# Gated linear attention by groups of tokens with projections as three rounded products, and low levels of a recurrence as 64-column tiles

## The reference

```
# HGRN2: per head, b = cumsum(log_f) in a chunk
scores[t, s] = sum_k q[t, k] * exp(b[t, k] - b[s, k]) * k[s, k]   for s <= t
o = scores @ v + (q * exp(b)) @ S
S = S * exp(b_last)[:, None] + (k * exp(b_last - b)).T @ v

# GLA, chunks of 64 tokens: u = h @ w_in
log_a = log_sigmoid(glr @ gate_up + bias) / 16        # glr: 16 columns of u
b = cumsum(log_a);  q_in = q * exp(b);  k_in = k * exp(-b);  k_st = k * exp(b_last - b)
scores = where(causal, q_in @ k_in.T, 0)
o = scores @ v + q_in @ S;   S = S * exp(b_last) + k_st.T @ v
out = o * rsqrt(mean(o * o) + eps) * norm_w * silu(g)
```

## Time and profile before

| | us |
|---|---|
| median of 3 runs | 4200.08 (4197.79 to 4201.01) |
| profiled execution | 4198.82, its span 4197.5 |
| PE busy | 3830.7 (91%) |
| DVE, ACT, POOL busy | 2019.6, 1521.5, 985.8 |
| mean granted clock of TensorE | 0.962 |

### The profile page before, as it was taken

One profiled execution on the slowest core, in us unless ns is written; L12 is line 12 of the kernel. 1 busy time (PEld: TensorE's weight loads), 2 busy tenths in 40 slices (PEclk: granted clock), 3 DMA queues, 4 the chain that ended last, 5 costly groups with the idle time before them and its releaser, 6 DMA issues.

```text
span 4197.5 us, 73047 instructions
## 1 busy us (share of the span) xinstructions
PE 3830.7 (91%) x30496; PEld 2853.2 (68%) x30496; DVE 2019.6 (48%) x4533; ACT 1521.5 (36%) x2905; POOL 985.8 (23%) x1018
## 2 busy tenths in 40 slices
PE   7999979896999998999997969999999979999989
PEld 4565558685877877878776857776777754655567
DVE  4665552354555555555553346666665651222222
ACT  3444441222444444444443334444444321122132
POOL 0000001232444443444432232322222200000032
PEclk9999989998999999999998989999999989999889
DMA  3000000222101101010103321111111120010032
GB/s 120 22 1 1 1 16 26 85 86 72 36 26 32 30 27 30 25 36 26 31 11 125 131 86 40 37 43 37 38 42 37 38 95 22 0 31 1 0 116 90
DMA packets 186549, 183.36 MB, mean 44 GB/s; under 512 B 6496, under 2 KB 158320, under 8 KB 186224
## 3 DMA queue, kind: packets, MB, share of 16 engines
q1 hardware_dynamic: 186224, 178.69, 13.4%
HBM read 145.12 MB, written 33.55 MB: 43 GB/s over the span
## 4 chain that ended last, share of the span: by engine, by line
PE 80%; DVE 9%; ACT 6%; issue 2%; DMA 2%; POOL 1%; SPq 0%; ACTq 0%; DVEq 0%; POOLq 0%
PE bank L193 15%; PE bank L195 14%; PE bank L194 14%; PE bank L1598 6%; PE bank L1169 4%; PE bank L447 4%; ACT arena L187 3%; PE bank L1655 3%; PE bank L2071 2%; DVE arena L685 1%; PE bank L2082 1%; ACT L277 1%; DVE arena L178 1%; PE bank L487 1%; PE bank L1698 1%
## 5 line engine op out<-in xcount | busy, mean ns | idle before, releaser
L194 PE MATMUL bank<-hT_cut,arena_cut 128*128 128x512 f32 x1824 | 725.3, 398 | 0.0
L187 ACT ACTIVATE arena<-bank 128x512 f32<-128x512 f32 (+1 forms) x584 | 313.0, 569 | 970.9 <-PE bank L195 450.8
L187 ACT ACTIVATE arena<-arena 128x512 f32<-128x512 f32 (+3 forms) x690 | 359.3, 549 | 283.8 <-POOL arena L1352 221.3
L193 PE MATMUL bank<-hT_cut,arena_cut 128*128 128x512 f32 x920 | 424.7, 462 | 8.9 <-DVE hT_cut L1409 8.9
L194 PEld LDWEIGHTS bank<-hT_cut,arena_cut 128*128 128x128 f32 x1824 | 351.2, 193 | 68.3 <-issue 15.2
L188 ACT ACTIVATE arena<-arena 128x256 f32<-128x256 f32 (+2 forms) x336 | 210.1, 626 | 511.6 <-DVE arena L177 276.6
L195 PE MATMUL bank<-hT_cut,arena_cut 128*128 128x512 f32 x920 | 366.5, 398 | 0.0
L193 PE MATMUL bank<-arena_cut,hT_cut 128*128 128x512 f32 x768 | 308.5, 402 | 61.4 <-POOL oT_cut L949 61.4
L2340 POOL TENSOR_TENSOR arena_cut<-arena,arena_cut 128x256 fp32r<-128x256 f32 x272 | 224.0, 854 | 477.6 <-ACT arena_cut L187 477.6
L193 PE MATMUL bank<-oT_cut,arena_cut 128*128 128x512 f32 x648 | 289.4, 447 | 44.3 <-POOL arena_cut L2340 23.0
L194 PE MATMUL bank<-arena_cut,hT_cut 128*128 128x512 f32 x768 | 305.8, 398 | 0.0
(11 more groups left out here) (222 smaller groups left out, 7244.2 us busy)
## 6 DMA issues: line engine op xcount, KB each, us to landing
arena<-in_w_in SPq DMA_DIRECT2D x72, 512.0 KB, 3.8
arena<-in_rec_w_in SPq DMA_DIRECT2D x64, 512.0 KB, 4.1
x_after<-arena SPq DMA_DIRECT2D x32, 512.0 KB, 2.6
arena<-x_after SPq DMA_DIRECT2D x32, 512.0 KB, 4.1
oT<-in_x SPq DMA_DIRECT2D x16, 512.0 KB, 3.6
arena<-in_x SPq DMA_DIRECT2D x16, 512.0 KB, 3.6
h_after<-hT SPq DMA_DIRECT2D x4, 2048.0 KB, 7.7
hT<-h_after SPq DMA_DIRECT2D x4, 2048.0 KB, 16.8
```

The lines of the kernel that those rows point to most:

```text
L187: return e.activation(out, a, f, bias=bias, scale=scale)
L193: pe.matmul(out, a[0], b[0], start=start, stop=False)
L194: pe.matmul(out, a[0], b[1], start=False, stop=False)
```

## The change

In `recurrence` the diagonal and the levels 0 to 5 are cut into tiles of 64 output rows: eight matmuls in place of four, each with 64 columns of weights, on the left and the right half of the array in turn (`own`). Level 6 stays.

`gla` is written anew around the same arithmetic. Units run over groups outside and pairs of heads inside. All projections are `product`s; the weights come in blocks of 128 columns (z0, z1, k, q) through three places, v in one wide piece, and every unit loads, rounds (ACT) and subtracts (POOL) them again. The tokens of a group are split once, at its first unit (ACT rounds, DVE subtracts into `hT_cut`). The gate product stands first in the front and has 128 rows, the low-rank product is made one group ahead on four column quarters. Scores are 64 x 64 tiles copied by a mask; the output's inner part (L1736) and its state part (L1744) are separate runs over both heads. `in_turn` has ten rounds with a fixed number of front ticks each. Of the diff, cut to its core:

```diff
             pe.wait_ge(*Fv.by("k", u))
             if before is not None:
                 pe.wait_ge(*taken_back(*before))
-            for j in range(4):
-                sl = slice(j * P, (j + 1) * P)
-                ins = pe.matmul(b[:, sl], kk[:, sl], q[:, sl], start=True, stop=True)
+            for i in range(8):
+                own, sl = slice(i % 2 * CH, (i % 2 + 1) * CH), slice(i * CH, (i + 1) * CH)
+                ins = pe.matmul(b[own, sl], kk[:, sl], q[:, sl], start=True, stop=True)
             ins.then_inc(*Bpe.did("diag"))
             yield
             for l in range(LEVELS):
@@ -1164,10 +1164,15 @@
                     pe.wait_ge(*Bv.by(f"e2_{l}", u))
                 if before is not None:
                     pe.wait_ge(*taken_back(*before))
-                for j in range(4):
-                    sl = slice(j * P, (j + 1) * P)
-                    ins = pe.matmul(b[:, j * CH:(j + 1) * CH], e[:, sl], view(e[:, sl], H)[:, :, 1, :],
-                                    start=True, stop=True)
+                for i in range(4 if H == CH else 8):
+                    if H == CH:
+                        sl = slice(i * P, (i + 1) * P)
+                        ins = pe.matmul(b[:, i * CH:(i + 1) * CH], e[:, sl], view(e[:, sl], H)[:, :, 1, :],
+                                        start=True, stop=True)
+                    else:
+                        own, sl = slice(i % 2 * CH, (i % 2 + 1) * CH), slice(i * CH, (i + 1) * CH)
+                        ins = pe.matmul(b[own, i * CH // 2:(i + 1) * CH // 2], e[:, sl], view(e[:, sl], H)[:, :, 1, :],
+                                        start=True, stop=True)
                 ins.then_inc(*Bpe.did(f"l{l}"))
                 yield
             b, before = kb.take("kt", u)
...
+    w_at = [k.room_cut(2 * KC * P) for _ in range(3)]
+    raw = [x[0].rearrange("p (s c n) -> p s c n", s=2, c=KC)[:, 0] for x in w_at]
+    w_lo, w_hi = ([x[1].rearrange("p (s c n) -> p s c n", s=2, c=KC)[:, s] for x in w_at] for s in range(2))
...
     def in_turn(front, back):
+        rounds = 10
         run(front(0))
         for u in range(UN):
-            merge((front(u + 1) if u + 1 < UN else None, 19), (back(u), 14))
+            late, ahead = back(u), front(u + 1) if u + 1 < UN else iter(())
+            ticks, went = 49 + (8 if u % 2 else 0), 0
+            for n in range(rounds):
+                next(late, None)
+                while went * rounds < (n + 1) * ticks:
+                    next(ahead, None)
+                    went += 1
+            run(late)
+            run(ahead)
...
+        def load(n):
+            u, kind = n // 4, kinds[n % 4]
+            if n >= 3:
+                sp.wait_ge(*Fpe.by(kinds[(n - 3) % 4], (n - 3) // 4))
+            c0, by = first_col[kind]
+            sp.dma_start(raw[n % 3], k.columns_of(w_in, c0 + units[u][1] * by, P)).then_inc(*w_got[n % 3].did("in"))
...
-        def lows():
-            pe.wait_ge(*g_got[0].by("in"))
-            for g in range(NG):
-                b = bank("low", g)
-                gen = project(b, wg, 0, g, m=16)
-                while True:
-                    try:
-                        next(gen)
-                    except StopIteration as done:
-                        done.value.then_inc(*l_pe.did("low"))
-                        break
+        def lows(g):
+            b = bank("low", g)
+            if g == 0:
+                pe.wait_ge(*g_got.by("in"))
+            for c in range(KC):
+                r = slice(32 * (c % 4), 32 * (c % 4) + 32)
+                ins = pe.matmul(b[r, :], wg[:, c, :], k.hT[:, c, cols_of(g)], start=(c < 4), stop=(c >= 4))
+            ins.then_inc(*l_pe.did("low"))
+
+        def block(kind, u):
+            g, p = units[u]
+            n = index(kind, u)
+            b = bank(kind, u)
+            pe.wait_ge(*w_p.by("lo", n))
+            for c in range(KC):
+                if kind == "z0" and p == 0:
+                    pe.wait_ge(*h_v.by("lo", g * KC + c))
+                ins = product(pe, b, (w_hi[n % 3][:, c, :], w_lo[n % 3][:, c, :]), (hi_of(g, c), lo_of(g, c)),
+                              start=(c == 0), stop=(c == KC - 1))
+                if c == KC - 1:
+                    ins.then_inc(*Fpe.did(kind))
+                yield
...
+                for r in range(4):
+                    pe.wait_ge(*u_got[r].by("in"))
+            pe.matmul(b, up[:, p * P:(p + 1) * P], low, start=True, stop=True).then_inc(*Fpe.did("g"))
+            yield
+            yield from block("z0", u)
+            yield from block("z1", u)
+            yield from block("k", u)
+            if p == 1 and g + 1 < NG:
+                lows(g + 1)
+            yield from block("q", u)
+            pe.wait_ge(*wv_p.by("lo", u))
+            for n in range(2):
+                b = bank(f"v{n}", u)
                 for j in range(2):
-                    t0 = g * G + (2 * half + j) * P
+                    t0 = slice((2 * n + j) * P, (2 * n + j + 1) * P)
                     for c in range(KC):
-                        ins = pe.matmul(b[:, j * 256:(j + 1) * 256], k.hT[:, c, t0:t0 + P], w_at["v"][:, c, :],
-                                        start=(c == 0), stop=(c == KC - 1))
-                        if c == 3:
+                        ins = product(pe, b[:, j * 256:(j + 1) * 256], (hi_of(g, c)[:, t0], lo_of(g, c)[:, t0]),
+                                      (v_hi[:, c, :], v_lo[:, c, :]), start=(c == 0), stop=(c == KC - 1))
+                        if j == 1 and c == KC - 1:
+                            ins.then_inc(*Fpe.did(f"v{n}"))
+                        if c % 2:
                             yield
-                ins.then_inc(*Fpe.did(f"v{half}"))
-            yield
 
...
             outs = [back_bank(f"o{h}", u) for h in range(2)]
+            pe.wait_ge(*Bv.by("s1", u))
+            for h in range(2):
+                for j in range(4):
+                    pe.matmul(outs[h][:, j * P:(j + 1) * P], vvv(u)[:, j, h * P:(h + 1) * P], sc_at[h][:, j * P:(j + 1) * P],
+                              start=(j == 0), stop=False)
+            yield
+            yield
             pe.wait_ge(*Bv.by("st8", u))
+            for i in range(8):
+                t0 = slice(i * CH, (i + 1) * CH)
+                for h in range(2):
+                    ins = pe.matmul(outs[h][:, t0], s3[half(h), i, :], q_at[u % 2][half(h), t0], start=False, stop=(i == 7))
+            ins.then_inc(*Bpe.did("o"))
+            yield
+            yield
             for h in range(2):
-                rows = slice(64 * h, 64 * h + 64)
-                for j in range(4):
-                    sl = slice(j * P, (j + 1) * P)
-                    pe.matmul(outs[h][:, sl], vvv(u)[:, j, h * P:(h + 1) * P], sc_at[h][:, sl], start=True, stop=False)
-                    for c in range(2):
-                        t0 = j * P + c * CH
...
+        lows(0)
         in_turn(front, back)
 
     def on_act():
+        def split(n):
+            if n < BN:
+                a.wait_ge(*w_got[n % 3].by("in", n // 3))
+                if n >= 3:
+                    a.wait_ge(*Fpe.by(kinds[(n - 3) % 4], (n - 3) // 4))
+                act(a, w_hi[n % 3], raw[n % 3], ACT.Copy).then_inc(*w_a.did("hi"))
+
+        def block(kind, u, mid={}):
+            for c in range(KC):
+                if c == 4:
+                    split(index(kind, u) + 1)
+                if c in mid:
+                    mid[c]()
...
+            def gate():
+                a.wait_ge(*Fpe.by("g", u))
+                if u:
+                    a.wait_ge(*Fv.by("z1", u - 1))
+                act(a, t1, fb.at("g", u), ACT.Abs, bias=bias[:, p:p + 1]).then_inc(*Fa.did("abs"))
+                a.wait_ge(*Fa.by("abs", u))
+                act(a, t1, t1, ACT.Exp, scale=-1.0).then_inc(*Fa.did("ex"))
+                a.wait_ge(*Fa.by("ex", u))
+                k.ln(t1, t1, bias=1.0).then_inc(*Fa.did("lp"))
+
...
+                    a.wait_ge(*Bv.by("st8", u - 2))
+                act(a, eb_at[u % 2], b_at, ACT.Exp, scale=1.0 / 16).then_inc(*Fa.did("eb"))
...
+                act(a, en, b_at, ACT.Exp, scale=-1.0 / 16).then_inc(*Fa.did("en"))
...
+            if p == 0:
+                if g in (1, 2):
+                    a.wait_ge(*Fpe.by("v1", u - 1))
+                for c in range(KC):
+                    act(a, hi_of(g, c), k.hT[:, c, cols_of(g)], ACT.Copy).then_inc(*h_a.did("hi"))
                     yield
...
+            gate()
+            yield
+            yield from block("z0", u, {3: decays, 6: last_decay})
...
+        def split(n):
+            if n < BN:
+                pool.wait_ge(*w_a.by("hi", n))
+                for c in range(0, KC, 2):
+                    ins = pool.tensor_tensor(w_lo[n % 3][:, c:c + 2, :], raw[n % 3][:, c:c + 2, :], w_hi[n % 3][:, c:c + 2, :], ALU.subtract)
+                ins.then_inc(*w_p.did("lo"))
+
+        def block(kind, u, mid={}):
+            for c in range(KC):
+                if c == 4:
```

(35 more changed lines are left out.)

366 lines of the change are left out of this document (189 added, 177 removed).

## The result

| | before | changed |
|---|---|---|
| median, us | 4198.93 (4197.32 to 4201.01, 4 runs) | 4071.32 (4062.90 to 4074.21, 4 runs) |
| ratio, 95% interval | | 0.9694 (0.9680 to 0.9708) |
| profiled execution, us | 4198.82 | 4071.80 |

A forecast was written before the change was run, and what follows sets the result against it. PE, busy 91% of the span, was taken as the bound. GLA's -65 (rounds), -16 (start) and -11 (end) made -92, the recurrence -15: -107 in all, so 4092 us, range 4040 to 4145.

The forecast's parts named there:

- The recurrence, -15 taken: First recurrence: seven tiled groups in 32 units at 0.816 us for 0.887, 16 us, taken as 15 for slack on PE.
- The rival with the whole factor of two: First recurrence: column halves halve its groups, 0.44 us for 0.887, gaining 99 us instead of 15: 4008; chance 0.03.
- The rival without overlap: First recurrence: column halves do not overlap with 128 rows, losing 88 us instead of gaining 15: 4195; chance 0.03.
- v at 0.125 a record: GLA's v projection: 96 rounded 256-column records at 0.125 us each, 12.0 us a unit.
- The fp32 price: GLA's v before the change: 128 x 256 fp32 products at 0.43 us each, 64 records in 13.81 us.
- The rival with slow narrow products: GLA's v: narrow rounded products no cheaper than fp32, 0.43 us each, 41 us a unit instead of 12: 4326; chance 0.04.
- The walk: GLA rounds, engine by engine: PE waits for z1 3.1 us in odd and 7.5 us in even rounds.
- The 2.3 us for q in the even rounds: GLA even rounds: POOL's queue of splits for k, v and q makes q 2.3 us late.
- Clock, 0.4 and 1.7 us taken: GLA rounds: reduced clock after PE's waits charged at 0.4 us in odd and 1.7 us in even rounds.
- the forecast of 49.3 and 55.8: GLA's odd and even round lengths in us, with 0.6 unassigned in each: seven take 365 against 430, 65 less.
- PE never late, 4040: GLA rival: splits ready in time as ACT and POOL run ahead, taking 52 us more off; chance 0.14.
- Start -16, end -11: GLA's start takes 59 us instead of 75, 16 less; the last unit's rest 17 instead of 28, 11 less.

The follow-up runs named there:

- e1: Changed kernel with the first recurrence as before (8 records of 128-wide weights a group), GLA as changed: 4087.7 us, ratio 0.9741.
- e3: Changed kernel with the tile records of levels 0 to 5 issued twice in a row, halves in alternation: 4153.9 us, ratio 0.9899.
- e9: Changed kernel with the recurrence's diagonal issued directly before level 0, one change of tiling fewer a unit: 4052.8 us, ratio 0.9658.
- e12: Changed kernel with the recurrence on the whole array as before and levels 0 to 5 issued twice: 4260.0 us, one execution.
- e2: Changed kernel with each recurrence group's eight left-half records first, then the eight right-half ones, instead of alternating: 4127.1 us, ratio 0.9834.
- e11: e2 with levels 0 to 5 issued twice, sixteen left-half records and then sixteen right-half ones: 4299.9 us, one execution.
- e7: Changed kernel with v's products in fp32 again (64 records a unit) instead of three rounded products (96 records): 4086.2 us, ratio 0.9736.
- e4: Changed kernel with ACT's rounding and POOL's subtractions for z1 and k issued during v of the unit before: 4036.3 us, ratio 0.9619.
- e5: e4 with POOL's eight subtractions for v put behind the four for q: 4020.1 us, ratio 0.9574.
- e10: e5 with GLA's starting transfers reordered, ACT's first roundings of h not behind the table's arrival, and e9's diagonal order: 4004.6 us, ratio 0.9541.
- e8: Changed kernel with the low-rank product's eight fp32 products one after another on one column quarter, instead of four quarters: 4079.6 us, ratio 0.9720.

## Why the prediction held, step by step

- **The recurrence, -15 taken, -22.0 measured.** The mechanism is right (e1); the term was mis-sized. The diagonal costs the 0.816 us that the earlier trace rows gave (0.814), a level with 32 moving columns 0.787, and PE was always the one that is late, so the 1 us taken off for that was wrong too: (6 x 0.100 + 0.073) x 32 = 21.5. Of its two parts, 0.35 for the change of tiling and 0.058 a step of two tiles, e3 gives 0.32 and 0.058. That the 0.32 us comes with the change of tiling is shown by e9, where one change fewer takes 0.35 us away. The Trainium skill (TensorEngine Tiling (Array Packing), Key Properties) states the drain at a change of mode; e12 shows no such part without tiles, so the trace agrees.
- **The rival with the whole factor of two** fell by exactly that part: without it, the records alone cost 0.467 against 0.894, nearly the 2x, but 16 short ones can't spread 0.32 us. **The rival without overlap** fell too; e2 and e11 show when it would hold. The Trainium skill (TensorE: Matmul & The Clock Gate, Part 3: Packing small matmuls, The mechanism) says that loads of weights overlap with running matmuls only when the row group differs; just before, it also allows a load into a background buffer. All records here use all 128 rows, so by the first sentence alone nothing would overlap. But the diagonal before pays nothing for 64 more moving columns, which by the 0.232 us of 512 would take 0.03, so its loads do run beside its matmuls. Whether the 0.029 us in alternation are a load beside a matmul of the other half or two loads side by side is not shown. The Trainium skill (TensorE: Matmul & The Clock Gate, LDWEIGHTS (loading the stationary operand)) gives a load's ns as its columns divided by 1.2, from which I estimate 107 ns for 128 columns and 53 for 64; the 0.112 and 0.058 us a record lie 5 ns above, so the trace agrees.
- **v at 0.125 a record, 0.1135 to 0.118 measured:** 0.9 us a unit, 7 in all, too dear. The fp32 price was right (e7). The rival with slow narrow products decided at 0.26; it is far off.
- **Waits in the rounds.** The walk named the right waits: 2.5 for 3.1 us in the odd rounds, 6.8 for 7.5 in the even ones. It was too long by POOL's price (2.79 instead of 3.26 us for four pieces), and in the even rounds the scan ended after 14.2 us, not 15.6, as DVE's score copies take 1.33 instead of 1.9. The 2.3 us for q in the even rounds did not come; they come when z1 no longer waits (e4). L1736's wait of 1.2 us was missed.
- **Clock, 0.4 and 1.7 us taken, 1.7 and 2.9 measured.** The stretches at half clock are 3.4 us in odd rounds, all of it with PE at work, and 10.2 in even ones, 5.7 of it at work. I had taken the 1.7 us behind the wait of 4.17 us in the earlier trace rows for the even rounds and guessed the odd ones. The stretch is no fixed price: e1 and e9 have the same waits of 6.8 us as the changed kernel, but stretches of 6.8, 6.8 and 10.2 us, and even rounds of 52.0, 52.9 and 53.3 (in e9 53.2).
- **The rounds add up:** odd 44.37 (e5) + 2.65 + 1.7 = 48.7; even 43.67 + 6.96 + 2.9 = 53.5 (waits here from start to start). In the forecast of 49.3 and 55.8 the waits in the even rounds (10.4, of which 2.3 for q never came), the dear v and the 0.6 us left unassigned outweighed the cheap clock: 65 instead of 73.6 us. That the two round lengths came so near is in part luck, as errors of both signs met in them.
- **PE never late, 4040:** it did not hold in the changed kernel. e5 is that case made nearly real (waits of 1.2 and 1.5 us are left): 48.1 us off the rounds, and 4020.
- **Start -16, end -11:** -19.6 and -12.6. The size at the start is in part luck. The walk has 5 us of waits for the first splits, 9 for z1 and 4.5 for q; measured are 0.5, 6.4 and 1.1, and 3.5 for the gate's second weights, which it did not have: 7 us less in all. PE's first record comes 6.3 us after the delta rule's last, before 7.2. Against that stands a term that the walk had put at nothing: some 10.6 us of PE's work at the start run at a granted clock of 0.5 (before 2.7), which costs about 5 us.

## What to carry to other kernels

Price a short group of tiles as a fixed part for the change of tiling (here 0.32 us) and a part for each record set by its columns of weights, halved throughout only if neighbouring records alternate between column halves; then put tile groups next to one another before cutting anything finer. When operands are split by other engines just before PE needs them, walk each engine's list in order: the split that stands behind a dependent chain is late. Moving it earlier cost nothing here (e4), but once it was gone the queue showed the next late one (e5 put that right). Count a wait of PE twice, once for itself and once for the half-clock work that follows, and count the latter only while PE is at work.

## What was not expected of the hardware

- A level's records on 64 columns cost 0.058 us on one column half and 0.029 in alternation, but with all of one half first only about four records overlap (1.040 and 1.974 us for 16 and 32 records).
- Rounded records of 256 columns ran at 0.1135 us in one unit and 0.118 in the next, steadily; why is open.
- In e5's and e10's rounds, where PE is busy 302 of 308 us and waits 1.5 us at most, the granted clock stayed at 2.4 GHz throughout. In the changed kernel it fell to 1.2 GHz once in each round, behind the wait of 2.65 us in the odd ones and within that of 6.96 us in the even ones, for 3.4 and 10.2 us. The same long wait came with 6.8 us in e8 and in two of the three even rounds of e1 and of e9; what decides between the lengths is open.
